# A new tile order, packed modulation weights, earlier delta-rule gates and row-tiled gate spreads in a two-layer hybrid backbone

## What is computed

```
for i in range(2):
    shift, scale, gate (two of each) = split(silu(c) @ mod_w[i] + mod_b[i], 6)   # also for c_ctx
    h = modulate(rmsnorm(x), shift, scale)
    m = mixer_ab(h, ...) if i == 0 else mixer_cd(h, ...)
    x = x + g1 * m
    x = x + g2 * expert_choice_ffn(modulate(rmsnorm(x), ...))
mixer_cd:
    ga, gb, q, k, v, og, a_raw, b_raw = split(h @ w_in + b_in)       # 49 column tiles of 128
    glu  = ga * sigmoid(gb)              # then a depthwise conv of 31 taps, LayerNorm, swish
    q, k, v = silu(dwconv3(q, k, v));  q, k = l2norm(q) * 128**-0.5, l2norm(k)
    beta, logg = sigmoid(b_raw), -exp(a_log) * softplus(a_raw + dt_bias)
    gated delta rule, 8 heads, forward and backward, in chunks;  merge, output projection
```

## Time and profile before

| | |
|---|---|
| profiled execution | 2334.64 us, its span 2332.7 us |
| median of three runs | 2334.65 us |
| TensorE matmul busy | 1962.0 us (84%) |
| VectorE, ScalarE, GpSimd busy | 721.2, 497.5, 164.7 us |
| HBM read | 524.26 MB, 225 GB/s over the span |

### The profile page before, as it was taken

The page is one execution under the profiler, slowest core; times in us unless marked ns, Lnnn a source line. Parts: engine busy times, 40 slices in busy tenths (PEclk is TensorE's granted clock), DMA queues, the critical chain, the costliest instruction groups (busy, mean ns, idle before and its releaser), DMA issues.

```text
span 2332.7 us, 29851 instructions
## 1 busy us (share of the span) xinstructions
PE 1962.0 (84%) x12790; PEld 1014.4 (43%) x12790; DVE 721.2 (31%) x1302; ACT 497.5 (21%) x1066; POOL 164.7 (7%) x208
## 2 busy tenths in 40 slices
PE   5999789999997998889898988889998776666655
PEld 2444544445443333333335655568887521212112
DVE  2121543335314001010116855766774300000001
ACT  2432312233102100000014322244432100000001
POOL 0000000020000000000004000044440000000000
PEclk9999989999998999999999999999998877878788
DMA  9112121250125999999992253300001489999996
GB/s 370 50 64 75 78 110 63 77 222 1 37 72 252 396 430 431 431 431 430 431 406 92 91 216 153 144 3 2 2 2 75 178 377 431 431 432 431 431 432 258
DMA packets 57810, 527.21 MB, mean 226 GB/s; under 512 B 2896, under 2 KB 4176, under 8 KB 43088
## 3 DMA queue, kind: packets, MB, share of 16 engines
q1 hardware_dynamic: 56064, 522.55, 53.9%
q10 hardware_dynamic: 1616, 2.76, 0.3%
HBM read 524.26 MB, written 1.05 MB: 225 GB/s over the span
## 4 chain that ended last, share of the span: by engine, by line
PE 48%; DMA 30%; DVE 7%; issue 6%; PEld 4%; ACT 2%; DVEq 1%; SPq 1%; PEldq 1%; ACTq 0%; POOL 0%
DMA ring<-in_moe_w 28%; PE bank L512 15%; PE bank L1063 10%; PE bank L973 5%; PEld bank L512 3%; PE bank L934 2%; DVE ring L1880 2%; PE bank L715 2%; PE bank L738 2%; DMA ring<-in_cd_w 1%; DVE x L2285 1%; DMA ring<-in_ab_w 1%; PE bank L564 1%; PE bank L662 1%; SPq L305 1%
## 5 line engine op out<-in xcount | busy, mean ns | idle before, releaser
L512 PE MATMUL bank<-hT,ring 128*128 128x512 f32 (+1 forms) x1504 | 553.5, 526 | 24.5 <-DMA ring<-in_cd_w 12.0
L1063 PE MATMUL bank<-ring,xgs 128*32 128x512 f32 x3072 | 394.4, 668 | 141.7 <-DMA ring<-in_moe_w 140.4
L512 PEld LDWEIGHTS bank<-hT,ring 128*128 128x128 f32 x1504 | 286.1, 193 | 272.5 <-issue 238.8
L1063 PEld LDWEIGHTS bank<-ring,xgs 128*32 128x32 f32 x3072 | 110.4, 121 | 399.8 <-issue 298.1
L1063 PE MATMUL bank<-ring,hT 128*32 128x512 f32 x1488 | 200.2, 694 | 75.7 <-DMA ring<-in_moe_w 75.7
L2126 DVE SCALAR_TENSOR_TENSOR x<-bank,modT,x 128x256 f32<-128x256 f32 x96 | 42.4, 481 | 468.2 <-PE bank L1089 468.2
L1063 PEld LDWEIGHTS bank<-ring,hT 128*32 128x32 f32 x1488 | 56.2, 125 | 206.6 <-issue 163.9
L1733 DVE SCALAR_TENSOR_TENSOR x<-gluR,cols,x 128x256 f32<-128x256 f32 x240 | 116.1, 484 | 17.0 <-issue 1.7
L2115 DVE TENSOR_TENSOR hT<-mrow,bank 128x512 f32<-128x512 f32 x16 | 11.0, 685 | 190.9 <-PE bank L1063 190.9
L2115 DVE TENSOR_TENSOR hT<-small,bank 128x512 f32<-128x512 f32 x8 | 5.5, 688 | 180.1 <-PE bank L1063 180.1
L1478 ACT ACTIVATE xgs<-bank 128x512 f32<-128x512 f32 x24 | 14.3, 597 | 210.2 <-PE bank L1046 210.2
(11 more groups left out here) (473 smaller groups left out, 2338.9 us busy)
## 6 DMA issues: line engine op xcount, KB each, us to landing
ring<-in_moe_w SPq DMA_DIRECT2D x94, 4096.0 KB, 22.5
ring<-in_mod_w SPq DMA_DIRECT2D x48, 1024.0 KB, 11.9
ring<-in_cd_w SPq DMA_DIRECT2D x6, 4096.0 KB, 17.3
ring<-in_ab_w SPq DMA_DIRECT2D x5, 4096.0 KB, 21.7
ring<-in_ab_wo SPq DMA_DIRECT2D x2, 4096.0 KB, 14.9
ring<-in_cd_wo SPq DMA_DIRECT2D x2, 4096.0 KB, 13.1
early<-in_moe_w SPq DMA_DIRECT2D x2, 2048.0 KB, 21.7
ring<-in_moe_w SPq DMA_DIRECT2D x2, 2048.0 KB, 18.3
```

Source lines behind the costliest of these rows:

```text
L512: last = mm(ps[p["no"] % 4][:, p["c0"]:T], w[:, k, :], hT[:, k, p["c0"]:T], start=(k == 0), stop=(k == KD - 1))
L1063: last = mm(ps[banks + s][32 * j:32 * j + 32, :], lhs[s][:, 4 * kh + k, 32 * j:32 * j + 32], w[:, 4 * k + j, :], start=(kh == 0 and k == 0 ...
```

## The change

- **Tile order of the layer-1 projection:** small, gb0, ga0, then for i of 0 to 7: gb(i+1), ga(i+1), k, v, q, og. `glu_at` becomes a list, since the taps of two blocks can fall on one tile.
- **Modulation weights** are laid out on the host so that each group is one transfer of 4 MB with 32 KB per partition. `CD_MODS` goes from {3: 1, 4: 2} to {2: 1, 4: 2}.
- **First projection group of layer 0** is fetched in two transfers: two tiles with a semaphore of their own, then six.
- **Gates:** their transposes go to the place before tile 28, the copies to VectorE's tile 29, the exps to ScalarE's tile 30, the sign to VectorE's tile 32. The norms' roots are split: heads 0 to 5 in tiles 42 to 45; for heads 6 and 7 the last squares come at the end of iteration -1, the sum and the root in iteration 0, the scaling in iteration 1 of the delta rule.
- **Spreads:** both directions in one place, behind `state_step(s, 0)`, each on 32 rows of `gcb`, at row tiles 0 and 32.
- GpSimd waits for the last projection group before it clears `Yt`.

The diff, cut to its core:

```
-CD_ALL = [("small", 0)] + [(k, i) for i in range(8) for k in ("gb", "ga", "k", "v", "og", "q")]
+CD_ALL = [("small", 0), ("gb", 0), ("ga", 0)]
+for _i in range(8):
+    CD_ALL += [(k, _i + 1) for k in ("gb", "ga") if _i < 7] + [(k, _i) for k in ("k", "v", "q", "og")]
-CD_MODS = {3: 1, 4: 2}
+CD_MODS = {2: 1, 4: 2}
-        return [(f"mod{layer}{r}", i, 4) for i in range(2)]
+        return [(f"mod{layer}{r}", i, 1) for i in range(2)]
...
-                for g in range(4):
-                    cb = 4 * r + g
-                    sp.dma_start(ring[:, s, g, :].rearrange("p (k n) -> p k n", k=4),
-                                 w[:, 4 * i:4 * i + 4, 512 * cb:512 * cb + 512]).then_inc(landed[s], 16)
+                sp.dma_start(ring[:, s, :, :].rearrange("p g n -> p (g n)"), A["mod_w"][layer, r, i]).then_inc(landed[s], 16)
...
+                if stage == "gla" and i == 0:
+                    sp.dma_start(... [:, 0:2, :], w[0:2] ...).then_inc(first_tiles, 16)
+                    sp.dma_start(... [:, 2:8, :], w[2:8] ...).then_inc(landed[s], 16)
+                    return
...   (TensorE)
+                if j == 28:
+                    gdn_gates()
                 if j % 8 == 0 and j // 8 in CD_MODS:
+                    if j > 28:
+                        pe.wait_ge(sg("gate_gap"), 2)
                     modulation_rows(1, CD_MODS[j // 8])
...
-                def spread(n, d):
+                def spreads(n):
                     if n > 0:
+                        pe.wait_ge(sg("gdn_S"), 2 * n)
+                        pe.wait_ge(sg("gdn_aqk"), n)
-                    mm(ps[4 + d], ident[:, n + 32 * d:n + 32 * d + 1].broadcast_to([P, P]), gcb,
-                       start=True, stop=True).then_inc(sg("gdn_spr"), 1)
+                    for d in range(2):
+                        r = slice(32 * d, 32 * d + 32)
+                        mm(ps[4 + d], ident[r, n + 32 * d:n + 32 * d + 1].broadcast_to([32, P]), gcb[r, :],
+                           start=True, stop=True, tile_position=(32 * d, 0)).then_inc(sg("gdn_spr"), 1)
...
                     level_r(p, 1)
                     new_values(s, 0)
-                    spread(n, 0)
                     level_p(p, 1)
                     state_step(s, 0)
-                    spread(n, 1)
+                    spreads(n)
...   (ScalarE)
+                if j == 30:  (exps)      j == 42:  drain, kq_squared     j == 44:  wait root_in 4, Sqrt of heads 0 to 5
...
+                    if it == -1:
+                        (squares of k7 and q7);  act.drain().then_inc(sg("kq_squared"), 1)
+                    if it == 0:
+                        act.wait_ge(sg("root_in"), 5)
+                        A_(rkq[:, 6:8, :], rkq[:, 6:8, :], ACT.Sqrt).then_inc(sg("root_out"), 1)
...   (VectorE)
+                    outputs(s)
+                    if it == 0:
+                        key_sums(slice(6, 8), 2)
+                    if it == 1:
+                        key_scales(slice(6, 8), 5)
```

More of the change, by code:

```diff
@@ L689, in gdn_gates @@
                 pe.wait_ge(sg("gate_cums"), 2)
-                pe.wait_ge(sg("proj_evacuated"), sum(len(made) for made in PLAN.values()))
-                pe.wait_ge(sg("turn_copied"), counts["turn"])
+                pe.wait_ge(sg("mod_added"), 5)
                 for t in range(NT):
-                    nc.tensor.transpose(ps[0][:, t * P:(t + 1) * P], gcb[:, t * P:(t + 1) * P], ident[:, :])
-                mm(ps[1][:, 0:256], ones[:, :], albuf2, start=True, stop=True).then_inc(sg("gate_cums_turned"), 1)
+                    nc.tensor.transpose(ps[7][:, t * P:(t + 1) * P], gcb[:, t * P:(t + 1) * P], ident[:, :])
+                mm(ps[6][:, 0:256], ones[:, :], albuf2, start=True, stop=True).then_inc(sg("gate_cums_turned"), 1)
             def gdn():
@@ L1177, in _ @@
             experts(0, (0, 1))
-            project(PLAN["cd"], ready=2 * KD, between=modulation_between)
-            gdn_gates()
+            project(PLAN["cd"], ready=2 * KD, between=cd_between)
+            pe.wait_ge(sg("turn_copied"), counts["turn"])
+            pe.wait_ge(sg("proj_evacuated"), sum(len(made) for made in PLAN.values()))
             gdn()
@@ L1243, in gla_softplus, with kq_squares @@
                 A_(gl, gu, ACT.Ln, bias=1.0).then_inc(sg("gla_lnz"), 1)
-            def project(made, dest, conv_bias=None, gates=False, between=None):
[L1246 to L1252, removed]
+            def kq_squares(p):
+                act.wait_ge(sg("turn_copied"), p["turn"] + 1)
+                first, v = (0, k_t) if p["kind"] == "k" else (4, q_t)
+                act.drain()
+                for t in range(NT if first == 0 else 2):
+                    A_(mrow[:, t * P:t * P + P], v[:, p["i"], t, :], ACT.Square, accum_out=rkq[:, p["i"], first + t:first + t + 1])
+            def project(made, dest, conv_bias=None, gates=False, between=None):
                 def finish_conv(p):
@@ L1440, in gdn @@
                     conformer_squares(it, range(6, 8))
+                    if it == -1:
+                        for p in PLAN["cd"]:
+                            if p["kind"] in ("k", "q") and p["i"] >= 6 and p["no"] + 4 > PLAN["cd"][-1]["no"]:
+                                kq_squares(p)
+                        act.drain().then_inc(sg("kq_squared"), 1)
+                    if it == 0:
+                        act.wait_ge(sg("root_in"), 5)
+                        A_(rkq[:, 6:8, :], rkq[:, 6:8, :], ACT.Sqrt).then_inc(sg("root_out"), 1)
                     if it == KD - 1:
-                        act.wait_ge(sg("root_in"), 5)
+                        act.wait_ge(sg("root_in"), 6)
                         A_(rstd[:, 0:SEQ], rstd[:, 0:SEQ], ACT.Sqrt).then_inc(sg("root_out"), 1)
@@ L1779, in project @@
                         gla_gated(0, 0, 0)
-                    if j in glu_at:
-                        conformer_taps(*glu_at[j])
+                    for steps in glu_at.get(j, []):
+                        conformer_taps(*steps)
                     if between is not None:
```

105 lines of the change are left out of this document (61 added, 44 removed).

## The result

The kernel after takes 2342.14 us (median of 20 runs, 2335.44 to 2347.45); the kernel before took 2335.1 beside it. The ratio is 1.0027, interval 1.0021 to 1.0034: 0.27% slower, small but clear of the scatter, where the forecast was 2332.4 and the range ended at 2340. The profiled execution took 2337.86 us, its span 2336.1 against 2332.7. It is one of the quicker of a kernel whose runs lie 12 us apart, so the trace shows 3.4 us of a median loss of about 7; of the rest it says nothing.

What follows compares the result with a forecast made beforehand. Bound by the chain of waits, 48% TensorE and 30% DMA. Start -4.2, projection with tail -2.0 and delta rule +4.0 gave -2.2 from 2334.64, so 2332.4 us; range 2328 to 2337, with the rivals 2324 to 2340.

Steps and rivals of the forecast that it cites:

- The start, -4.2: Kernel start: second modulation group arrives 2.1 us earlier, first two tiles end at about 55; -4.2 us, bounds -2.1 to -6.5.
- The first 16 tiles, +8.2: Layer-1 projection: VectorE's overlapping taps make TensorE wait for transposes of v0, q0, v1, q1; +8.2 us, bounds 0 to 10.
- The two smaller waits (0.65, 0.9): Layer-1 projection, first 16 tiles: VectorE still late for v1 and q1, costing 0.65 and 0.9 us.
- Weight waits, -1.6: Layer-1 projection, tiles 16 to 48: both waits stay, the first becomes like the second; -1.6 us, bounds 0 to -2.8.
- Gate transposes, +0.9: Layer-1 projection, before tile 28: the gates' transposes now stand in TensorE's queue; +0.9 us, bounds 0 to 2.1.
- The tail, -9.5: Last projection tile to the delta rule's first level: S+14.1 us instead of 23.6; -9.5 us, bounds -6 to -11.5.
- The paired spreads: Delta rule heads: the pair hides behind VectorE's copy, ScalarE has 0.48 us spare; 0, bounds 0 and +0.3 a head.
- Rival 2: Delta rule: gaps around the short pair lower TensorE's clock in each of seven heads; +10.5 us, 2342.9 us, chance 0.13.
- The roots of heads 6 and 7, +3.2 and +0.8: Delta rule: ScalarE's wait for VectorE's sum in iteration 0, +3.2 us; scaling in VectorE's critical block in iteration 1, +0.8.

Runs made afterwards that it cites:

- e6: The kernel before with only the packed modulation weights and the divided first projection group; 2331.33 us, ratio 0.9983 to the kernel before.
- e5: The kernel after with the spreads back in their two old places, each still on 32 rows; 2338.41 us, ratio 1.0016 to the kernel before.
- e1: The kernel after with the old spreads, 128 rows in the two old places; 2329.39 us, ratio 0.9975 to the kernel before.
- e7: e1 with the sum, root and scaling of heads 6 and 7 moved into gaps; 2331.51 us, ratio 0.9986 to the kernel before.
- e9: The kernel after, paired spreads kept, with sum, root and scaling of heads 6 and 7 moved into gaps; 2337.5 us, ratio 1.0007 to the kernel before.
- e3: The kernel after with both spreads in the new place but on 128 rows; 2336.75 us, ratio 1.0005 to the kernel before.

## Why the prediction was wrong, point by point

- **The start, -4.2: right.** 4.8 in the trace, 3.8 by e6's median; the first L523 at 39.72 for a forecast of 40.0. The mechanism (second modulation group earlier, then ScalarE's pace) is in the rows. The size varies with the clock: in e6 the modulation rows take 3.64 us instead of 5.06, and its first projection product starts at 38.29.
- **The first 16 tiles, +8.2: the waits right, the sum in part by luck.** 2.25 and 4.08 us came for 2.3 and 4.3, at the tiles named. The two smaller waits (0.65, 0.9) did not come: 6.3. In their place stand 1.7 us of lowered clock in the four tiles behind the second wait, which the forecast did not have.
- **Weight waits, -1.6: right.** 5.34 and 5.18 for 6.37 and 5.67, less 0.2 and plus 0.6 in the tiles behind them: -1.2. **Gate transposes, +0.9: right,** 0.87 from 1384.21 to the next tile at 1385.08. The projection's sum was 7.5 and came out at 8.2; these terms and the slow tiles make 7.7 of it.
- **The tail, -9.5: too large by 2.3.** With S for the end of the last tile, S+14.1 was forecast, S+16.4 came. The decays began at S+3.2, forecast S+3.0. Behind them lie 13.2 us, not the 11.1 of the forecast. The old 11.2 and the table load of 1.28 make 12.5. I had taken 1.4 off because the transposes would no longer run at half clock behind a wait. They do, and more of them than before (granted clock 0.61 for 0.81 over the stretch, 3.37 us for L796's 16 matmuls where before they took 2.85), so 0.7 came on top instead. The wait for the decays just ahead (3.76 us) is the likely reason; no run tests it. The table load took the 1.28 of the row. What "ScalarE: Activation LUTs" of the Trainium skill (What ACT_TABLE_LOAD costs) gives, about 2.66, none of these runs shows.
- **The paired spreads, "their gain is 0 ... I take 0; bounds 0 and +0.3 a head, 2 in all": this step failed.** The work itself did what was said: the pair takes 1.13 us and hides behind VectorE. A lone 32-row product takes 1.12 (e5), so the second rides along for 0.01. "TensorE: Matmul & The Clock Gate" of the Trainium skill (Measured speedup vs the span model) states just that for row tiles, some 4 ns for each further one, and the trace agrees. But the term counted only the path and not the clock. With the old spreads back (e1) the heads take 10.3 us less in the profile and the program 12.7 less by the medians, far outside the bound of 2.
- **Rival 2: the right cause, the right number in part by luck.** It said that the new spreads' gaps lower the clock, +10.5, and 2342.9; 2342.14 came. But it had 1.5 us in each of seven heads, and level 2's R over 1.5 us in each. Of the 10.3 us, 4.8 are in head 1 and 2.6 in head 2, 1.3 each in heads 4 and 6, 0.2 in head 0, and heads 3, 5 and 7 have none. Its chance of 0.13 rested on one row: a gap of 1.13 us a head kept the clock at 1.00. That row had the two long products next to the gap, which the change took away; it spoke of the kernel before only.
- **The roots of heads 6 and 7, +3.2 and +0.8: mis-sized, and it depends.** At full clock they cost 1.6 and 0.4 (e1 against e7). With the pair they cost 3.2 in head 1 (35.2 against e9's 32.0), 4.6 in the median. The mechanism, VectorE's sum ahead of ScalarE's copy, is in the rows.
- **Range.** The prediction's 2324 to 2340 is called the range "with the rivals", yet leaves out rival 2's own 2342.9. With the spreads at 0 the terms sum to -2.2, and e1, which has all of the change but the spreads, came out at -6.1, e7 at -3.6, both inside 2324 to 2340. The failed step alone puts the time outside.

## What to carry to other kernels

Before making a product smaller, look at what it does for TensorE's clock: in a stage with small matmuls and short waits, redundant rows in idle time can be the cheaper choice. Here 2.0 us of full-height products became 1.1 us of low ones off the critical path, and the heads became 10.3 us longer. A long wait passed alone (e1), a shorter-rowed product and a new place passed alone too (the settled heads of e5 and e3), and together they lower the clock, so try such edits together and apart; and read the granted clock of each repetition of a loop, not only its length. Of this change the start is worth keeping (the packed weights and the divided first group, which no run here separates), with the old spreads. The fastest kernel here, 2329.39 us (e1), has both; of its other parts no run shows a gain.

## What the runs showed of the hardware that I had not expected

- The same place, the same wait, nearly the same product time (1.02 and 1.12 us), with 128 or with 32 rows: full clock behind the one, half clock behind the other (e1, e5).
- The same program can scatter by half a per cent: 12.0 us between the extremes in 20 runs of the kernel after, against 4.8 in 20 of the kernel before and 4.3 in 9 of e1. The half-clock stretches fall in other places from one execution to the next, and nine kernels with the same start reach the layer-1 projection up to 6.0 us apart. So one profiled execution can lie several microseconds from the median, and a term of 2 us, like e7's against e1, is below what these runs can tell.
- Two transfers of 4 MB with 32 KB rows occupy SP for 1.05 us, the eight of 1 MB with 2 KB rows for 20.11, at 433 and 387 GB/s.
